# Prompt attention in a hybrid decoder step: split operands, values by four heads, gate and mix rows by tile

## The reference, cut to what matters

```python
q = rms_norm(q_down, q_norm) @ w_uq              # 384 -> 16 heads x 96; 32 of the 96 get the rotary turn
k_nope = jnp.einsum('btc,chn->bthn', c_kv, w_uk)  # 256 -> 16 heads x 64
v = jnp.einsum('btc,chv->bthv', c_kv, w_uv)       # 256 -> 16 heads x 64
s = (jnp.einsum('bqhn,bkhn->bhqk', qn_b, k_nope) + jnp.einsum('bqhr,bkr->bhqk', qr_b, k_rope)) * MLA_SCALE
s = jnp.where(key_pos[None, :] <= q_pos[:, None], s, NEG_BIG)
p = jax.nn.softmax(s, axis=-1)
o = jnp.einsum('bhqk,bkhv->bqhv', p, v)           # then times sigmoid(gm), added to the other branch
```

## Time and profile before

| | |
|---|---|
| time before, median of 3 runs | 2600.66 us (2597.71 to 2602.58) |
| the profiled execution | 2591.6 us, span 2589.8 us |
| busy share of the span | PE 91%, PEld 70%, DVE 51%, ACT 39%, POOL 25% |
| prompt attention in that execution | from about 1107 to about 1645 us |

### The profile page before, as it was taken

One profiled execution on the slowest core, in us unless ns is written; L12 is line 12 of the kernel. 1 busy time (PEld: TensorE's weight loads), 2 busy tenths in 40 slices (PEclk: granted clock), 3 DMA queues, 4 the chain that ended last, 5 costly groups with the idle time before them and its releaser, 6 DMA issues. The chain is left out here.

```text
span 2589.8 us, 46955 instructions
## 1 busy us (share of the span) xinstructions
PE 2358.8 (91%) x18273; PEld 1804.9 (70%) x18273; DVE 1324.3 (51%) x2529; ACT 1017.2 (39%) x2036; POOL 656.3 (25%) x716
## 2 busy tenths in 40 slices
PE   6999999999799999789999999799997995999980
PEld 6999999999788888635656556666663554666660
DVE  6365664333157777334555556344442435666655
ACT  5157751132122323314544545343441113665652
POOL 0100000011135454323333331244440111222210
PEclk9999999999879999989999999899998996999995
DMA  4222233334245353140000100467674502999865
GB/s 146 82 66 73 83 104 105 107 129 145 90 127 148 97 151 92 42 135 1 26 26 26 41 35 10 156 243 270 240 273 131 214 28 90 342 355 347 333 258 214
DMA packets 178645, 361.23 MB, mean 139 GB/s; under 512 B 36596, under 2 KB 128200, under 8 KB 157945
## 3 DMA queue, kind: packets, MB, share of 16 engines
q1 hardware_dynamic: 145609, 225.01, 25.8%
q0 software_dynamic: 32848, 133.56, 13.6%
HBM read 302.91 MB, written 72.18 MB: 145 GB/s over the span
## 5 line engine op out<-in xcount | busy, mean ns | idle before, releaser
L136 PE MATMUL pi_acc<-hT_hi,pi_w_hi 128*128 128x352 f32 (+1 forms) x1152 | 378.7, 329 | 0.0
L136 PE MATMUL pi_acc<-hT_lo,pi_w_hi 128*128 128x352 f32 (+1 forms) x1152 | 371.8, 323 | 0.0
L136 PE MATMUL pi_acc<-hT_hi,pi_w_lo 128*128 128x352 f32 (+1 forms) x1152 | 371.7, 323 | 0.0
L2791 DVE TENSOR_TENSOR ex_w_lo<-w_raw,ex_w_hi 128x512 fp32r<-128x512 f32 x256 | 160.0, 687 | 120.7 <-ACT ex_w_hi L2759 120.7
L136 PEld LDWEIGHTS pi_acc<-hT_hi,pi_w_hi 128*128 128x128 f32 x1152 | 217.6, 189 | 4.0 <-issue 3.8
L136 PEld LDWEIGHTS pi_acc<-hT_lo,pi_w_hi 128*128 128x128 f32 x1152 | 217.4, 189 | 4.0 <-issue 3.8
L136 PEld LDWEIGHTS pi_acc<-hT_hi,pi_w_lo 128*128 128x128 f32 x1152 | 217.3, 189 | 0.0
L2759 ACT CAST ex_w_hi<-w_raw 128x512 fp32r<-128x512 f32 x256 | 140.1, 617 | 100.4 <-DMA w_raw<-w_up 49.7
L1654 PE MATMUL at_sc<-at_keyT,at_qT 96*128 96x512 f32 (+5 forms) x480 | 161.1, 443 | 3.2 <-POOL at_qT L1584 2.3
L1910 ACT ACTIVATE at_p<-at_sc,at_nm 16x16 f32<-16x16 f32 (+5 forms) x144 | 100.7, 699 | 155.3 <-DVE at_nm L1773 154.2
L1771 DVE TENSOR_REDUCE at_mx<-at_sc 16x1 f32<-16x16 f32 (+5 forms) x144 | 101.3, 704 | 96.2 <-PE at_sc L1658 95.3
(11 more groups left out here) (509 smaller groups left out, 4931.0 us busy)
## 6 DMA issues: line engine op xcount, KB each, us to landing
w_raw<-w_gate SPq DMA_DIRECT2D x32, 1024.0 KB, 8.7
w_raw<-w_up SPq DMA_DIRECT2D x32, 1024.0 KB, 12.0
wd<-w_down SPq DMA_DIRECT2D x32, 1024.0 KB, 6.3
pi_piece<-w_in SPq DMA_DIRECT2D x64, 384.0 KB, 3.3
projT<-pi_xr POOLq DMA_DIRECT2D x24, 524.0 KB, 3.2
convT<-pi_yn POOLq DMA_DIRECT2D x24, 512.0 KB, 2.9
gp_heads<-convT SPq DMA_DIRECT2D x8, 1536.0 KB, 8.6
gp_zg<-projT SPq DMA_DIRECT2D x16, 512.0 KB, 5.3
```

The costliest lines, as they stand in the source:

```text
L136: last = nc.tensor.matmul(out, lhs[a], rhs[b], start=(start and i == 0), stop=(stop and i == 2))
L2791: nc.vector.tensor_tensor(w_lo[:, c, :].rearrange("p (j f) -> p j f", j=2), raw[:, i, :, c * DE:(c + 1) * DE], w_hi[:, c, :].bitcast(F32). ...
```

## The change

The fp32 products of `make`, `make_values` and `scores` become three one-pass products of split operands each (the new helper `three`), and what they read is split somewhere:

- the latents in the opening, by tile: ScalarE casts `lat_hi`, VectorE subtracts `lat_lo`;
- the weights of queries and keys by pair: ScalarE casts (`weights_hi`), GpSimd subtracts (`weights_lo`, at unit 12 for the pair after the next). The query weights are loaded anew for each pair;
- the queries by tile on GpSimd: `split_queries(w)` casts both heads' 128 rows (96 x 256) and subtracts, one tile ahead of the scores. TensorE waits for it (`q_lo_made`) ahead of a tile's first score;
- the keys: ScalarE makes two casts per half in place of the one copy, VectorE two subtractions that wait for them. GpSimd copies the key's rotary rows once, in the opening.

The mask's table and unit matrix become fp32r. Meta rows are computed as a full tile. The values are made for four heads at a time (`WIDE`, 256 columns) in three products: the first group in the opening, the other three in the loop, in pairs 0 to 5, at units 10, 12 and 14 of an even pair and 10 and 12 of an odd one; their weights are split by group. Gate and mix rows are loaded and stored by tile, in four buffers, three tiles ahead. In the opening, SyncE now loads the mask's table behind the latents' and weights' loads, and transposes, value sets and steps follow the table `OPENING`.

```diff
-    AHEAD, LATER = 3, 4
...
+    SET_AT = {10: 0, 12: 1, 14: 2}
...
+    OPENING = [("t", 0), ("t", 1), ("t", 2), ("t", 3), ("v", 0), ("t", 4), ("v", 1), ("s", 0), ("t", 5), ("t", 6), ("v", 2), ("t", 7), ("t", 8),
+               ("v", 3), ("v", 4)] + [("s", i) for i in range(1, STEPS)]
...
+        q_hi, q_lo = (s.sb(f"at_q_{n}", [QK, 2, 2, P], F32R) for n in ("hi", "lo"))
+        future, eye = s.sb("at_future", [P, P], F32R), s.sb("at_eye", [P, P], F32R)
...
+            return hp + 2 if i == 12 and hp + 2 < PAIRS else None
...
+            return hp // 2 + 1 if i == 5 and hp % 2 == 0 and hp // 2 + 1 < PAIRS // 2 else None
...
-                def load(hp):
-                    sp.dma_start(gm[:, hp % 2, NS:], d["projT"][GM0 + hp, :, NS:]).then_inc(pair_loaded[hp % 2], 16)
-                    sp.dma_start(mix[:, hp % 2, NS:], d["mixT"][hp, :, NS:]).then_inc(pair_loaded[hp % 2], 16)
+                def load(w):
+                    hp, t = divmod(w, NT)
+                    r0, n = CHUNKS[t]
+                    sp.dma_start(gm[:, w % 4, 0:n], d["projT"][GM0 + hp, :, r0:r0 + n]).then_inc(tile_loaded[w % 4], 16)
+                    sp.dma_start(mix[:, w % 4, 0:n], d["mixT"][hp, :, r0:r0 + n]).then_inc(tile_loaded[w % 4], 16)
...
+                def load_query_weights(hp):
+                    for c in range(KQ):
+                        sp.dma_start(w_raw[:, 2 * c:2 * c + 2, 0:QK], query_weights(hp)[:, c]).then_inc(wq_loaded, 16)
...
+                load_query_weights(0)
+                sp.dma_start(k.wuk[:], d["w_uk"][0].rearrange("(c p) h n -> p c (h n)", p=P)).then_inc(wk_loaded, 16)
...
+                sp.dma_start(tc[:, 0:P], d["c_future"]).then_inc(loaded, 16)
...
+                def split_queries(w):
+                    hp, t = divmod(w, NT)
+                    r0, slot = CHUNKS[t][0], 2 * (hp % 2)
+                    mine = qT[0:QK, slot:slot + 2, r0:r0 + P]
+                    start_wide()
+                    if t == 0:
+                        pool.wait_ge(roped, 5 * (hp + 1))
+                    if w >= 2:
+                        pool.wait_ge(scored, 2 * w - 2)
+                    nc.gpsimd.tensor_copy(q_hi[:, w % 2], mine).then_inc(q_hi_made, 1)
+                    pool.wait_ge(q_hi_made, w + 1)
+                    nc.gpsimd.tensor_tensor(q_lo[:, w % 2], mine, q_hi[:, w % 2].bitcast(F32), ALU.subtract).then_inc(q_lo_made, 1)
+                    wide[:] = [(q_lo_made, w + 1)]
...
+                    nc.gpsimd.tensor_tensor(w_lo[:, 0:2 * KQ], w_raw[:], w_hi[:, 0:2 * KQ].bitcast(F32), ALU.subtract)
+                    nc.gpsimd.tensor_tensor(w_lo[:, 2 * KQ:], k.wuk[:, :, cols], w_hi[:, 2 * KQ:].bitcast(F32), ALU.subtract).then_inc(w_lo_made, 1)
...
+                    nc.gpsimd.tensor_tensor(wv_lo[:], k.wuv[:, :, g * WIDE:(g + 1) * WIDE], wv_hi[:].bitcast(F32), ALU.subtract).then_inc(wv_lo_made, 1)
...
                 for step in (0, 1, 2, 3, 6):
                     turn_rope(0, step)
+                split_queries(0)
...
+                nc.gpsimd.tensor_copy(key_hi[NOPE:QK, 2:4, :], key_hi[NOPE:QK, 0:2, :].bitcast(F32))
+                nc.gpsimd.tensor_copy(key_lo[NOPE:QK, 2:4, :], key_lo[NOPE:QK, 0:2, :].bitcast(F32)).then_inc(ropes_copied, 1)
...
                 for u in range(U + 4):
                     if u >= 5 and u % 2 == 1:
                         mix_in((u - 5) // 2)
+                    if u % 2 == 0 and u // 2 + 1 < W:
+                        split_queries(u // 2 + 1)
...
+                    if u < U and weights_of(u):
+                        weights_lo(weights_of(u))
+                    if u < U and value_weights_of(u):
+                        value_weights_lo(value_weights_of(u))
...
+                def three(out, lhs, rhs, first, last, grouped=True):
+                    for i, (a, b) in enumerate(((0, 0), (0, 1), (1, 0))):
+                        ins = nc.tensor.matmul(out, lhs[a], rhs[b], start=(first and i == 0), stop=(last and i == 2), skip_group_check=not grouped)
+                    return ins
...
-                            last = nc.tensor.matmul(mid, k.wuq[:, c, 2 * hp + a, :], k.qlT[:, c, c0:c1], start=(c == 0), stop=(c == KQ - 1))
+                            last = three(mid, [v[:, 2 * c + a, :] for v in (w_hi, w_lo)], [v[:, 2 + c, c0:c1] for v in (lat_hi, lat_lo)], c == 0, c == KQ - 1)
...
-                        last = nc.tensor.matmul(scf[0:n, x:e], qT[0:QK, slot, r0:r0 + n], keyT[:, slot, x - base:e - base], start=True, stop=False, skip_group_check=True)
+                        last = three(scf[:, x:e], [v[:, w % 2, a, :] for v in (q_hi, q_lo)], [v[:, slot, x - base:e - base] for v in (key_hi, key_lo)], True, False, False)
...
                         make(*step_of(u))
+                    if u < U and set_of(u):
+                        make_values(*set_of(u))
...
-                            pe.wait_ge(roped, 5 * (hp + 1))
+                        if a == 0:
+                            pe.wait_ge(q_lo_made, u // 2 + 1)
...
+                    dve.wait_ge(mid_kept_a, STEPS * hp + step + 1)
...
+                    for a in range(2):
+                        last = nc.vector.tensor_tensor(key_lo[0:NOPE, slot + a, c0:c1], mid[a * NOPE:(a + 1) * NOPE, b0:b0 + c1 - c0],
+                                                       key_hi[0:NOPE, slot + a, c0:c1].bitcast(F32), ALU.subtract)
...
+                        if i == 0:
+                            dve.wait_ge(loaded, 16)
+                            nc.vector.tensor_copy(future[:], tc[:, 0:P])
+                            nc.vector.tensor_copy(eye[:], k.ident[:]).then_inc(eyes, 1)
...
+                    act.wait_ge(swapped, hp + 1)
+                    nc.scalar.copy(w_hi[:, 0:2 * KQ], w_raw[:]).then_inc(w_hi_made, 1)
...
+                        for a in range(2):
+                            last = nc.scalar.copy(key_hi[0:NOPE, slot + a, c0 - NS:c1 - NS], mid[a * NOPE:(a + 1) * NOPE, :])
```

More of the change, by code:

```diff
@@ L1455, in attend_prompt @@
+    MADE = [x for x in OPENING if x[0] != "t"]
+    with k.scope() as old:
+        kv_rest, q_rest = old.sb("at_kv_rest", [P, NT - LG, CK], side="right"), old.sb("at_q_rest", [P, NT - LG, QL], side="right")
+        stage = old.sb("at_stage", [P, 2, KL, P], side="right")
+    k.early.stack.close()
     with k.scope() as s:
-        val = s.sb("at_val", [P, NT, D])
+        p = s.sb("at_p", [P, 3, PROMPT], side="right")
+        pT = s.sb("at_pT", [P, 2, 2, NT, P], side="right")
+        val = s.sb("at_val", [P, 2, 2 * SETS, WIDE])
@@ L1548, in _ @@
                 sp.dma_start(place[:], d["c_place"]).then_inc(placed, 16)
[L1549 to L1556, removed]
+                for w in range(3):
+                    load(w)
@@ new lines, in _ @@
+                sp.wait_ge(mid_made, STEPS)
+                load_query_weights(1)
+                for w in range(W):
+                    hp, t = divmod(w, NT)
+                    r0, n = CHUNKS[t]
+                    sp.wait_ge(mixed, w + 1)
+                    sp.dma_start(d["mixT"][hp, :, r0:r0 + n], mix[:, w % 4, 0:n]).then_inc(tile_stored[w % 4], 16)
+                    if w + 3 < W:
+                        if w:
+                            sp.wait_ge(tile_stored[(w - 1) % 4], 16 * ((w - 1) // 4 + 1))
+                        load(w + 3)
+                    if t == 3 and hp + 2 < PAIRS:
+                        sp.wait_ge(mid_made, STEPS * (hp + 2))
+                        load_query_weights(hp + 2)
@@ L1624, in make @@
                         for c in range(2):
-                            last = nc.tensor.matmul(mid, k.wuk[:, c, hp * P:(hp + 1) * P], k.latT[:, c, c0:c1], start=(c == 0), stop=(c == 1))
+                            last = three(mid, [v[:, 2 * KQ + c, :] for v in (w_hi, w_lo)], [v[:, c, c0:c1] for v in (lat_hi, lat_lo)], c == 0, c == 1)
                     else:
@@ L1724, in _ @@
-                for step in range(NT - LATER, STEPS):
-                    make(0, step)
-                pe.wait_ge(v_kept_a, NT)
-                pe.wait_ge(v_kept_v, NT)
-                pe.wait_ge(eyes, 1)
+                for kind, i in OPENING:
+                    if kind == "t":
+                        turn_latents(i)
+                    elif kind == "v":
+                        make_values(0, i)
+                    else:
+                        make(0, i)
+                pe.wait_ge(v_kept, SETS)
@@ L1836, in _ @@
-                for step in range(NT - LATER, STEPS):
-                    take(0, step)
+                    nc.vector.tensor_copy(key_hi[NOPE:QK, 0:2, c0 - NS:r0 + n - NS], mine).then_inc(rope_hi, 1)
+                    if t >= 2:
+                        dve.wait_ge(lat_hi_made, t - 1)
+                    nc.vector.tensor_tensor(staged(t)[:, 2:, 0:n], tp[:, 1, 0:KQ, 0:n],
+                                            k.vecT[:, V_Q:V_GDN].unsqueeze(2).to_broadcast([P, KQ, n]), ALU.mult)
+                    dve.wait_ge(rope_hi, t + 1)
```

320 lines of the change are left out of this document (198 added, 122 removed).

## The result

| | median | range |
|---|---|---|
| before | 2599.2 us | 2594.8 to 2602.6 |
| changed | 2668.8 us | 2665.0 to 2670.4 |

The ratio is 1.0272, 95% interval 1.0253 to 1.0291: 70 us slower, where 42 had been forecast. The profiled execution took 2670.4 us, its span 2668.6.

A forecast was written before the change was run, and what follows sets the result against it. TensorE's work was taken to bound the attention loop before the change, with GpSimd's queue making it wait after. From 2600.7 us, -24 + 19 + 2 + 24 + 8 + 13 = +42 gave 2643 us, range 2605 to 2672.

The forecast's parts named there:

- TensorE's work: Prompt attention's loop: one-pass products save 24 us, value products moved in from the opening add 19, leaving 5 us less.
- The mask's +8: Loop: the longer weight load adds 0.05 us to each of 21 masks, 1.0 a pair, bounds 0 and 1.7.
- The opening: Before the second pair's first product: no shortening despite less TensorE work, +2 us, bounds -4 and +8.
- the chain that was named: Opening: VectorE waits for the late mask table, then eight tiles pass through VectorE and ScalarE at 3.2 us each.
- The stands: Fifth tile: TensorE waits 2.9 or 4.2 us for GpSimd's query split, +24; VectorE and ScalarE delays add 8.
- the sign: Changed profile: TensorE waits 2 to 4.5 us for GpSimd's low query part before fifth-tile scores in seven of eight pairs.
- The clock: Loop: TensorE's clock falls behind the new stands, costing 1.9 us a pair, +13, bounds 0 and 24.
- The nearest rival: Loop clock falls in every pair as long as at 1174, opening at its upper bound: 2660 us, chance 0.18.
- GpSimd keeps up: Loop: GpSimd's split ends in time, TensorE stays the bound: 2598 us, or 2578 with cheaper small products; chance 0.16.
- The stand alone: Fifth tile: TensorE stands without a clock drop, VectorE's chain hidden under it: +21, 2622 us, chance 0.27.
- products pay for their loads: Loop: weight loads do not overlap, some 138 products a pair each pay up to 0.19 us: 2800 us, chance 0.02.
- need more than one pass: Products at 96 rows or 256 columns do not run in one pass: some 100 us more, 2700 us, chance 0.02.

The follow-up runs named there:

- the run without stands: Changed kernel with queries split two tiles ahead, ScalarE copying step results first, and its weight cast one unit later: 2593.5 us, ratio 0.9993.
- two operations in the kernel before: Kernel before, plus two unread rope-sized GpSimd operations behind the fourth rope, which TensorE awaits ahead of the fifth tile: 2627.8 us, ratio 1.0120.
- the third try: Changed kernel with queries split two tiles ahead, ScalarE copying step results first, and VectorE's key subtractions behind the normalisation: 2638.9 us, ratio 1.0169.

## Why the prediction was right, and where not

Direction, place and range were right: slower, by GpSimd's split at the fifth tile, 2668.8 inside 2605 to 2672. The size was not: +70, not +42. That the range held is in part luck: with the measured price of the clock in its place the forecast's sum would be +81, or 2682, past the range, and it is less work and shorter stands than forecast that bring the time back inside.

- **TensorE's work.** Forecast -24 + 19 = -5 in the loop, pairs of 60.8 and 58.7 us where nothing is waited for; the run without stands has 59.7 and 58.1. Its loop is 7.0 us shorter than before, although TensorE waits 5.6 us more in it, so the work itself fell by some 12.5. The mask's +8 was too much.
- **The opening.** Forecast +2, measured +2.5, and by the chain that was named: the table came 13 us behind the first transposition (1113.57). That this chain could be moved out of the way was not seen.
- **The stands.** Forecast 2.9 and 4.2 us for GpSimd, +24, and +8 for VectorE and ScalarE. Measured: 1.35 to 2.64 for GpSimd in six pairs and 4.41 in the first, 15.5 together, since TensorE itself came late, by 1.0 us for VectorE in six pairs. That is below the bound of 20, and only three pairs have the 2 to 4.5 us that were named as the sign. All waits in the loop are 43.3 us against 15.0 before, +28 for the forecast's 32. The normalisations took 99.0 us in all, 84.6 before, +1.8 a pair. The Trainium skill's GPSIMD Engine Reference (Specifications) says that GpSimd shares its SBUF interfaces with VectorE where the latter runs in a two-port mode or has two SBUF inputs. The estimate by that rule was 2.6 a pair, and the trace agrees in kind: the normalisation of 1.52 us lies beside a rope.
- **The clock, the step that failed.** "I take 1.9 a pair, +13, bounds 0 and 24". Measured 52, by the difference to the run without stands. The forecast took the one drop in the trace of before, about 3 us lost behind a stand of 2.32, and made less of it. In the change the drop at the stands lasts 10 to 17 us in each of seven pairs, at half speed, and a short one behind the ninth tile's waits follows in most. That is some 7 us lost a pair, not 1.9, and outside the bound of 24 for all. The nearest rival, a drop in every pair "as long as at 1174", took that length too, and reached 2660.
- **The rivals.** "GpSimd keeps up" gave 2598 for its condition; with the condition made true the time is 2593.5. "The stand alone" (2622) needed a full clock, which the loop does not have. That products pay for their loads is out: full-height products start 0.23 us apart here too. That they need more than one pass is out as well: at full clock products of 96 rows and 512 columns start 0.23 us apart (1433.60 to 1433.83), those of 256 columns 0.12 (1432.24 to 1432.36).

The terms as measured, -12.5 + 2.5 + 28 + 52, make the +70 of attention.

## What to carry to other kernels

A stand of one or two microseconds in a loop that keeps TensorE full can cost several times its length, because the clock can fall with it and comes back late: look for the clock in every stretch behind a new wait on TensorE, and price the wait by what the stretch behind it costs at half speed, which was 3 to 17 us long here. Look also at what TensorE does just ahead of the wait. When work is split off onto an idle engine, its place in that engine's queue and the copies that feed it matter more than its busy time: here no work was removed, and 75 us came back by doing a split one tile earlier, a copy ahead of an exponential and a weight cast one unit later.

## What was not expected of the hardware

With two operations in the kernel before, stands of 1.15 to 1.22 us brought drops of 3.4 to 6.8 us in six pairs, and one of 1.88 us a drop of 10.2 in the first, while that kernel's own waits of 0.6 us bring none. But length alone does not decide. In the change TensorE waits 1.39 us for ScalarE's copied blocks in three pairs, longer than it does for VectorE at the fifth tile, and the clock stays full:

```profile
1439.31 0.93 PE L1811 MATMUL at_tp<-ident,at_p 128*16 128x128 f32 x7 [1.39 <-ACT at_pT L2055]
```

```profile
1438.00:1440.00 2.00, 0.69 (x8) 0.72 (x8) 1.09 (x2) 2.00 (x5) 1.27 (x1) 1.00 0.00 0
1440.00:1442.00 2.00, 2.00 (x16) 1.56 (x16) 1.60 (x3) 1.22 (x5) 2.00 (x4) 1.00 0.03 8
```

Five of the kernels have such waits, of 1.39 or 1.40 us, in three pairs each, and none of the fifteen brings a drop. Ahead of these waits TensorE makes score products of 272 and 512 columns; ahead of the stands at the fifth tile it makes the head step's small products, sixteen records of 24 and 16 columns, which bring no drop by themselves either (1377.44 to 1379.19, in a pair at full clock). So it may take both, the small products and a stand behind them; the prediction, too, had noted of its new stands that they "follow the same small matmuls". No run moved the head step away from the stand, so this is not shown.

Two waits of 1.5 us in the run without stands fit it: the one with a drop of 7 us comes behind waits of 0.3 and 0.4 us and products of 144 and 272 columns, the one with none behind products of 400 and 512. The waits of 1.53 us in the third try, with drops of 3.4 us, come 5 us behind the head step. What does not fit is that the ninth tile's waits of 0.4 and 0.5 us are followed by a short drop in most pairs of the change and by none in that run, and that drops behind like stands differ in length from pair to pair. What tells these apart stays open.
